# Deferring a fourth norm whose shift is carried as two extra columns, and 512-wide products in all three down projections

## The chip, the cores and the metric

The kernel runs on one core of one Trainium2 chip, in one launch. The metric is device time in microseconds (us), the median of several runs.

## What is computed

Two transformer-like blocks on x of 256 tokens by 1024 features, in fp32. The first block is a state-space mixer, a conv feed-forward (FFN 0), a differential attention and a second conv feed-forward (FFN 1). The second block mixes attention over chosen keys with a gated recurrence, and has a third feed-forward (FFN 2). What matters here is the start of the second block:

```python
mod = jnp.dot(c_act, w_ada[l]) + b_ada[l]
sh1, sc1, ga1, sh2, sc2, ga2 = [m[:, None, :] for m in jnp.split(mod, 6, axis=-1)]
xn = rms_norm_2(h, g_mix[l]) * (1.0 + sc1) + sh1
proj = jnp.dot(xn, w_in[l]) + b_in[l]
q, k, v, qi, ki, wi, xr, yr, gate_a, gate_b = jnp.split(proj, cuts, axis=-1)
```

and each feed-forward's last step, `(silu(gate) * up) @ down_w`, added to the residual stream.

## The kernel before

**Layout.** Activations stand by feature: x is 8 tiles of 128 features by 256 tokens. Every fp32 operand is split into a high and a low part in a reduced fp32 format, and one product of a weight tile (128 x 128) with an activation tile takes three matmuls into one PSUM bank (mm3, L865): low weights by high x, high weights by low x, high by high.

**Weights.** They stream in slabs of 128 x 2048 through a ring of three: SP loads a slab into raw, ScalarE (ACT) writes its high part wh (split_hi, L546, line 553), VectorE (DVE) the low part wl (split_lo, L555, line 567). A high split waits until TensorE (PE) has finished the slab three earlier; SP loads a slab when the low split of the slab three earlier is done. The order of slabs, products and PSUM groups is written out by hand in make_plan (L132) and once more in each engine's program; six PSUM banks are used in turn. Each engine runs its program in order and waits on semaphores.

**Norms.** A norm needs a sum of squares over all features, so over all tiles of x. In the plain form (norm_sum, L1066; norm, L1570 and L2257) PE waits for the sums, turns them into a factor for each token by two transposes (line 1057), and waits until DVE has made xn = x * gain * factor and ACT and DVE have split it. keep_busy matmuls (line 1029) fill part of the wait. In the deferred form (DEFERRED, L354: n1, n2, n3) the next projection runs on the split of x * gain, tile by tile as the residual sums come in (split_tiles, L2295); the sums (norm_squares, L1081, lines 1044 and 1048) and the transposes (norm_factor, L1088) stand among the projection's products, and DVE multiplies the projection's result by the factor.

**Around the change.** FFN 1 ends with the down projection dn1 (stream of kind PAIR3): 8 output tiles in 4 pairs, each pair 3 slabs of 8, 8 and 6 feature tiles, so 22 products for each output tile. residual3 (L2339) adds the results to x on DVE. Behind dn1 stands n4, which has a gain (gs1) and a shift (mod[0:8]) that come from the modulation sums; then the products kk, qi (two slabs, two_slabs takes kk and the first slab of qi together, L873), qi1, vw, qb, yr, xr and eight gate slabs, all from the split of n4's result in xh, xl. The modulation sums are 96 reductions on DVE (ada, L2233, line 2242), two for each step of the table ADA (L339), whose weights POOL loads through a small ring (modulation_weights, L777). In dn2, three of the four pairs already use a form with two matmuls for each product: a 512-wide one of the high weights by high and low activations side by side (line 959), and a 256-wide one of the low weights by the high activations (line 963); DVE adds both halves of the bank.

Of the kernel before, what the change touches and what calls it, by code (L numbers as in the profile page):

```python
# [13 lines left out]
F32 = mybir.dt.float32  # L14
# [324 lines left out]
ADA = {"so": 6, "dn0": 11, "v0": 1, "v1": 1, "v2": 1, "v3": 1, "ao": 2, "dn1": 11, "kk": 1, "qi": 2, "vw": 1, "woa": 2,  # L339
# [14 lines left out]
DEFERRED = {"n1": (1, "ffn_ln0"), "n2": (2, "kv_ln"), "n3": (4, "ffn_ln1")}  # L354
HALVED = ("xbc1", "xbc2", "up2+1")
XN_USES = {0: 0, 5: 1, 6: 2, 7: 3}
# [34 lines left out]
def build_program(nc, io, out):  # L391
    with ExitStack() as ctx:
# [14 lines left out]
        xh = sb("xh", [P, KD, T], F32R)  # L407
        xl = sb("xl", [P, KD, T], F32R)
# [58 lines left out]
        out_done = sem("out_done")  # L467
        (cact_done, ea_done, lam_done, spe_done, pre_done, conv_step, xbc_done, a_done,
# [185 lines left out]
        mh, ml = R(24 * T, 8, T), R(32 * T, 8, T)  # L654
# [13 lines left out]
        mod, gs1, gs2 = S(48), S(8), S(8)  # L668
        negc, posc = S(8), S(8)
# [87 lines left out]
        def _(pool):  # L757
# [78 lines left out]
            pool.wait_ge(xl_done, 8 * 6)  # L836
# [27 lines left out]
        def _(pe):  # L864
# [8 lines left out]
            def two_slabs(slabs, ready):  # L873

                for b, g in slabs:
                    pe.wait_ge(lo_done, b + 1)
                    acquire(pe, g)
                    acquire(pe, g + 1)
                for k in range(KD):
                    ready(k)  # L880
                    for b, g in slabs:
                        for t in range(2):
                            off = k * 256 + t * P
                            mm = mm3(bank(g + t)[:, 0:T],
                                     (wh[:, b % RING, off:off + P], wl[:, b % RING, off:off + P]),
                                     (xh[:, k, :], xl[:, k, :]), k == 0, k == KD - 1, False)
                            if k == KD - 1:
                                mm.then_inc(slab_done if t else half_done, 1)

            def stream(name, X, ready=None, between=None, late=None, deferred=None, factor=True):  # L890
# [6 lines left out]
                def stage(i, j):  # L897
# [37 lines left out]
                    for t in range(tiles):  # L935
# [14 lines left out]
                        if name == "dn2" and i < 3:  # L950
# [514 lines left out]
            for c in range(2):  # L1465
                for k in range(KD):
                    o = k * VW
                    mm = mm3(bank(g)[:, T * c:T * c + VW], (wh[:, b % RING, o:o + VW], wl[:, b % RING, o:o + VW]),
                             (xh[:, k, P * c:P * c + P], xl[:, k, P * c:P * c + P]), k == 0, k == KD - 1, True)
# [13 lines left out]
            for m in range(4):  # L1483
                slab_tile(f"qb{m//2}", m % 2)
# [35 lines left out]
            for s in range(4):  # L1520
                stream(f"yr{s}", (xh, xl))
            for s in range(4):
                stream(f"xr{s}", (xh, xl))
# [5 lines left out]
            for h in range(8):  # L1529
                slab_tile(gate_name(h), 0)  # L1530
# [3 lines left out]
                slab_tile(gate_name(h), 1)  # L1534
# [8 lines left out]
            ffn(2, "n5", 6, 5)  # L1543
# [4 lines left out]
        def _(act):  # L1548
# [11 lines left out]
            def square(r, m, g=None):  # L1560
# [7 lines left out]
                A(sq[:, m % 2, :], x[:, m, :], ACT.Square).then_inc(sq_done, 1)  # L1568

# [20 lines left out]
            def residual(name, r, n, last_of, to=None, first=0, whole=False):  # L1590

                A(warm, eps_t[:, :], ACT.Sqrt)
                for s in range(n + 1 if to else n):
                    if first <= s < (n if to or whole else n - 1):
                        hi(name, s)
                    if to:
                        for m, g in last_of(s - 1):
                            given_back(act, g)
                            A(xh[:, m, :], x[:, m, :], ACT.Copy, scale=vec(DEFERRED[to][1], m)).then_inc(xh_done, 1)
                            square(r, m, g)  # L1600
# [428 lines left out]
            ffn(1, "n3", [], {}, 3, None)  # L2029

            norm("n4", [5], {5: 0})
# [5 lines left out]
            hi("kk", 0)  # L2037
            g = PL.G["kk"]
            wait_tile(act, "kk", 0, 0, 0)
            k0, k1 = bank(g)[low_rows, 0:T], bank(g)[high_rows, 0:T]  # L2040
            biased(kkf[low_rows, 0, :], k0, vec("b_kk", 0)[low_rows, :])
            biased(kkf[high_rows, 0, :], k1, vec("b_kk", 1)[high_rows, :])
            biased(kkf[high_rows, 1, :], k0, vec("b_kk", 0)[low_rows, :])
            biased(kkf[low_rows, 1, :], k1, vec("b_kk", 1)[high_rows, :])
            act.wait_ge(qkv2_done, 4)
            act.sem_inc(free[g % PRING], 1)
            wait_tile(act, "kk", 0, 0, 1)
            biased(kif, bank(g + 1)[:, 0:T], vec("b_ki"))
            act.wait_ge(qkv2_done, 5)
            act.sem_inc(free[(g + 1) % PRING], 1)  # L2050
            for s in range(2):
                hi("qi", s)
                for t in range(2):
                    m, g = 2 * s + t, PL.G["qi"] + 2 * s + t
                    wait_tile(act, "qi", 0, s, t)
                    biased(qif[:, m, :], bank(g)[:, 0:T], vec("b_qi", m))
                    act.wait_ge(qkv2_done, 5 + m + 1)
                    act.sem_inc(free[g % PRING], 1)
# [158 lines left out]
            ffn(2, "n5", [6], {6: 24}, 5, ("wout", 3))  # L2217
# [4 lines left out]
        def _(dve):  # L2222
# [34 lines left out]
            def norm(name, use_gains, k, late=None, early=None):  # L2257
# [7 lines left out]
                for use, gain, shift in use_gains:  # L2265
# [10 lines left out]
                    for m in range(KD):  # L2276
                        V.scalar_tensor_tensor(xn[:, m, :], x[:, m, :], gain(m), bank(g)[:, 0:T],  # L2277
                                               ALU.mult, ALU.mult).then_inc(xn_done, 1)
                        if m and use < 7:
                            low(m - 1)  # L2280
                    if use < 7:
# [7 lines left out]
            def gained_low(use, gain, m, h_, l_):  # L2289

                dve.wait_ge(xh_done, 8 * use + m + 1)
                V.scalar_tensor_tensor(l_[:, m, :], x[:, m, :], vec(gain, m), h_[:, m, :].bitcast(F32),
# [1049 lines left out]
```

## Time and profile before

| | us |
|---|---|
| median of 3 runs | 1148.47 (1147.61 to 1148.58) |
| the profiled execution's own time | 1147.75 |
| its span (first to last instruction) | 1146.0 |
| PE busy in the span | 1127.0 |

The profiled execution takes 1.75 us more than its span and lies 0.72 us under the median of the runs. Line numbers are those of the kernel. A busy PE in these rows is modelled: matmuls are pipelined, and the step from one start to the next is what one costs.

### The profile page before, as it was taken

The page shows a single profiled execution, that of the slowest core. Times are in us where ns is not written, and L with a number is a line of the kernel's source. Part 1 is how long each engine was busy: PE and PEld are TensorE (multiplying, and loading weights), DVE is VectorE, ACT ScalarE, POOL GpSimd, SP SyncE. Part 2 cuts the span into 40 slices and gives each one's busy share as a digit, 9 for nine tenths or more (in the row PEclk, how much of TensorE's full clock was granted, in tenths as well). Part 3 has the DMA queues.
Part 4 walks back from the last instruction along what each step waited for, and adds up shares of the span by engine and source line. Part 5 has one row for each costly group of instructions (what it writes and reads, how often), then busy time and mean ns, then how long its engine had stood idle before and what let it go on. Part 6 is the DMA issues. An engine that isn't in the chain of part 4 may idle for free.

```text
span 1146.0 us, 24061 instructions
## 1 busy us (share of the span) xinstructions
PE 1127.0 (98%) x9194; PEld 1095.8 (96%) x9194; DVE 922.6 (81%) x1608; ACT 699.4 (61%) x1011; POOL 185.1 (16%) x233
## 2 busy tenths in 40 slices
PE   7999999999999999999999999999999999999997
PEld 6999999999999999999999999999988999999987
DVE  5899887788888878877888877679997769888784
ACT  5767885566665457875766653465876347666531
POOL 1000241011112200000111121101324101333310
PEclk9999999999999999999999999999999999999999
DMA  7465456655557864434555578575353655555570
GB/s 268 168 227 186 173 175 246 229 184 183 183 174 275 294 227 151 139 116 144 193 183 183 174 251 302 188 251 180 121 164 118 241 182 173 179 183 183 184 273 37
DMA packets 43713, 220.22 MB, mean 192 GB/s; under 512 B 8063, under 2 KB 12656, under 8 KB 22640
## 3 DMA queue, kind: packets, MB, share of 16 engines
q1 hardware_dynamic: 31552, 185.25, 46.7%
q0 software_dynamic: 9264, 30.94, 7.3%
q10 hardware_dynamic: 2816, 2.90, 0.8%
q8 instruction: 56, 0.92, 0.3%
q14 instruction: 25, 0.20, 0.1%
HBM read 217.97 MB, written 1.11 MB: 191 GB/s over the span
## 4 chain that ended last, share of the span: by engine, by line
PE 90%; DVE 6%; ACT 2%; issue 1%; DMA 0%; DVEq 0%; ACTq 0%
PE ps L870 77%; PE ps L959 3%; DVE wl L567 2%; PE ps L963 1%; ACT wh L553 1%; PE ps_idle L1029 1%; PE ps_idle L1139 1%; PE ps L1500 1%; DVE work L2277 1%; PE ps L1036 0%; DMA x<-in_x 0%; PE ps L1341 0%; PE ps L1477 0%; DVE work L2255 0%; PE ps L1475 0%
## 5 line engine op out<-in xcount | busy, mean ns | idle before, releaser
L870 PE MATMUL ps<-xh,wl 128*128 128x256 f32 x1776 | 509.3, 287 | 1.8 <-DVE xl L2272 1.1
L870 PE MATMUL ps<-xl,wh 128*128 128x256 f32 x1776 | 502.8, 283 | 0.0
L870 PE MATMUL ps<-xh,wh 128*128 128x256 f32 x1776 | 502.6, 283 | 0.0
L567 DVE TENSOR_TENSOR wl<-raw,wh 128x2048 fp32r<-128x2048 f32 (+1 forms) x175 | 394.6, 2256 | 69.6 <-ACT wh L553 68.9
L553 ACT ACTIVATE wh<-raw 128x2048 fp32r<-128x2048 f32 (+1 forms) x178 | 333.2, 1874 | 89.4 <-PE ps L870 69.8
L870 PEld LDWEIGHTS ps<-xh,wl 128*128 128x128 f32 x1776 | 340.7, 192 | 9.2 <-issue 6.7
L870 PEld LDWEIGHTS ps<-xl,wh 128*128 128x128 f32 x1776 | 340.8, 192 | 0.6 <-issue 0.5
L870 PEld LDWEIGHTS ps<-xh,wh 128*128 128x128 f32 x1776 | 340.7, 192 | 0.0
L870 PE MATMUL ps<-actr,wh 128*128 128x256 f32 x1624 | 293.0, 283 | 0.0
L870 PEld LDWEIGHTS ps<-actr,wh 128*128 128x128 f32 x1624 | 253.2, 192 | 0.0
L870 PE MATMUL ps<-actr,wl 128*128 128x256 f32 x812 | 231.3, 285 | 0.5 <-DVE wl L567 0.5
L870 PEld LDWEIGHTS ps<-actr,wl 128*128 128x128 f32 x812 | 155.7, 192 | 1.7 <-issue 1.0
L796 POOL TENSOR_TENSOR actr<-work,actr 128x256 f32 (+1 forms) x66 | 76.8, 1164 | 369.3 <-ACT actr L1855 369.3
L2437 DVE SCALAR_TENSOR_TENSOR work<-work,vecs 128x255 f32<-128x255 f32 (+2 forms) x200 | 85.0, 481 | 1.5 <-POOL work L843 0.9
L1864 ACT ACTIVATE work<-work,vecs 128x256 f32<-128x256 f32 x88 | 52.7, 601 | 38.2 <-DVE work L2702 38.2
L2437 DVE SCALAR_TENSOR_TENSOR work<-ps,vecs,work 128x255 f32<-128x255 f32 (+1 forms) x160 | 67.2, 473 | 10.0 <-ACT work L1864 9.3
L2702 DVE TENSOR_TENSOR work<-ps,work 128x256 f32<-128x256 f32 x88 | 36.9, 421 | 36.5 <-PE ps L870 36.5
L1850 ACT ACTIVATE work<-work 128x256 f32<-128x256 f32 x66 | 27.4, 415 | 54.6 <-DVE work L2437 54.6
L1568 ACT ACTIVATE work<-x 128x256 f32<-128x256 f32 x56 | 22.5, 409 | 56.6 <-DVE x L2369 21.2
L1864 ACT ACTIVATE work<-ps,vecs 128x256 f32<-128x256 f32 x44 | 24.7, 563 | 45.2 <-PE ps L870 45.2
L785 POOL DMA_DIRECT2D work<-in_w_ada x42 | 22.5, 537 | 173.5 <-DVE ada_sum L2242 172.6
L785 POOL DMA_DIRECT2D ada_w<-in_w_ada x54 | 29.1, 539 | 131.0 <-DVE ada_sum L2242 128.9
(279 smaller groups left out, 1231.7 us busy)
## 6 DMA issues: line engine op xcount, KB each, us to landing
raw<-in_up SPq DMA_DIRECT2D x66, 1024.0 KB, 4.9
ada_w<-in_w_ada POOLq DMA_DIRECT2D x54, 256.0 KB, 4.9
raw<-in_xbc SPq DMA_DIRECT2D x12, 1024.0 KB, 5.1
work<-in_w_ada POOLq DMA_DIRECT2D x42, 256.0 KB, 5.2
raw<-in_z SPq DMA_DIRECT2D x8, 1024.0 KB, 5.0
raw<-in_so SPq DMA_DIRECT2D x8, 1024.0 KB, 5.0
raw<-in_dn0a SPq DMA_DIRECT2D x8, 1024.0 KB, 4.9
raw<-in_dn1a SPq DMA_DIRECT2D x8, 1024.0 KB, 5.2
```

The lines of the kernel that those rows point to most:

```text
L553: nc.scalar.activation(wh[:, b % RING, 0:n], raw[:, b % RING, 0:n], ACT.Copy).then_inc(hi_done, 1)
L567: nc.vector.tensor_tensor(wl[:, b % RING, 0:n], raw[:, b % RING, 0:n], wh[:, b % RING, 0:n].bitcast(F32), ALU.subtract).then_inc(lo_done, 1)
L785: pool.dma_start(ada_ring[ada_slot(a)], io["w_ada"][a // 2][:, 512 * (a % 2):512 * (a % 2) + 512])\
L796: nc.gpsimd.tensor_tensor(dst, hbuf[:, j % RING, :], src.bitcast(F32), ALU.subtract)\
L870: mm = nc.tensor.matmul(o, l, r, start=start and n == 0, stop=stop and n == 2)
L959: return nc.tensor.matmul(bank(g), wh[:, r, off:off + P], both, start=k == 0, stop=last)
L963: return nc.tensor.matmul(bank(g)[:, 0:T], wl[:, r, off:off + P], X[0][:, k, :], start=False, stop=False)
L1568: A(sq[:, m % 2, :], x[:, m, :], ACT.Square).then_inc(sq_done, 1)
L1850: A(gsil[:, (j - 1) % RING, :], pre[:, 2 * ((j - 1) % RING), :], ACT.Silu)\
L1864: A(pre[:, 2 * (j % RING) + t, :], src, ACT.Identity, scale=vdyn(f"up_w{f}", 88 + 2 * s + t), bias=vdyn(f"up_b{f}", 2 * s + t))\
L2437: return V.scalar_tensor_tensor(dst[:, d:T], src[:, 0:T - d], w, dst[:, d:T], ALU.mult, ALU.add)
L2702: give_back(V.tensor_tensor(scaled[:, 2 * (j % RING) + t, :], bank(tile_group(up, j, t))[:, 0:T], rstd, ALU.mult), tile_group(up, j, t))
```

## The change

1. n4 is deferred. xh and xl get two more columns for each feature tile (pitch 258 instead of 256 values). kk and the first slab of qi run on the split of x * gs1 with the shift in column 256 (and 257), so that one product gives both the product of the tokens and that of the shift. DVE multiplies the former by the factor into `early` and adds the latter to the bias (early_tile); ACT then makes the same copies as before from there. n4's sums and transposes stand among kk's products.
2. The full n4 result is still made, as mixed (DVE), mixed_high (ACT) and mixed_low (DVE), into ch and cl; qi1, vw, qb, yr, xr and the gates read it there. What lay in that memory (mh, ml, the input of wout) goes to xh, xl.
3. The modulation sums for n4 (first_modulation) go from behind FFN 1 to behind the second weight split of dn1. Four reductions of step qi go to steps qb0 and yr0.
4. dn0 and dn1 take the form of dn2: in three of four pairs two matmuls for each product, and a second add on DVE.

```diff
-ADA = {... "dn1": 11, "kk": 1, "qi": 2, "vw": 1, "woa": 2,
+ADA = {... "dn1": 11, "kk": 1, "vw": 1, "qb0": 1, "yr0": 1, "woa": 2,
-DEFERRED = {"n1": (1, "ffn_ln0"), "n2": (2, "kv_ln"), "n3": (4, "ffn_ln1")}
+DEFERRED = {"n1": (1, "ffn_ln0"), "n2": (2, "kv_ln"), "n3": (4, "ffn_ln1"), "n4": (5, "gs1")}
...
-        xh = sb("xh", [P, KD, T], F32R)
-        xl = sb("xl", [P, KD, T], F32R)
+        xh_wide = sb("xh", [P, KD, T + 2], F32R)
+        xl_wide = sb("xl", [P, KD, T + 2], F32R)
+        xh, xl = xh_wide[:, :, 0:T], xl_wide[:, :, 0:T]
...
-        mh, ml = R(24 * T, 8, T), R(32 * T, 8, T)
+        ch, cl = R(24 * T, 8, T), R(32 * T, 8, T)
+        mh, ml = xh, xl
+        early = W(34 * KB, 4, T)
...
-            pool.wait_ge(xl_done, 8 * 6)
+            pool.wait_ge(xl_done, 8 * 7)
...
+            def shifted_tile(name, t, ready=None, ks=range(KD)):
...
+                    mm = mm3(bank(g)[:, 0:T + 2],
+                             (wh[:, b % RING, off:off + P], wl[:, b % RING, off:off + P]),
+                             (xh_wide[:, k, :], xl_wide[:, k, :]), k == 0, k == KD - 1, False)
...
-                        if name == "dn2" and i < 3:
+                        if kind == PAIR3 and i < 3:
...
-            norm_sum("n4", 4)
-            two_slabs(((PL.S["kk"], PL.G["kk"]), (PL.S["qi"], PL.G["qi"])), x_ready(5))
-            slab_tile("qi1", 0)
-            slab_tile("qi1", 1)
+            pe.wait_ge(shift_low, 1)
+            shifted_tile("kk", 0, x_ready(5))
+            shifted_tile("kk", 1, ks=range(0, 2))
+            norm_squares("n4", 4)
+            shifted_tile("kk", 1, ks=range(2, 6))
+            norm_factor("n4", 4)
+            shifted_tile("kk", 1, ks=range(6, 8))
+            shifted_tile("qi", 0)
+            shifted_tile("qi", 1)
+            slab_tile("qi1", 0, (ch, cl), x_ready(6))
+            slab_tile("qi1", 1, (ch, cl))
```

ACT behind dn1 (split_hi of a slab two ahead is written hi):

```diff
-            norm("n4", [5], {5: 0})
+            hi("kk", 0)
+            norm("n4", [])
+            for m in range(4):
+                mixed_high(m)
+            hi("qi", 0)
+            for m in range(4, KD):
+                mixed_high(m)
...
+            given_back(act, PL.G["kk"])
+            k0, k1 = early[low_rows, 0, :], early[high_rows, 0, :]
...
+            hi("qi", 1)
```

DVE:

```diff
-                                ins = V.tensor_tensor(x[:, m, :], bank(g)[:, 0:T], x[:, m, :], ALU.add)
+                                if p < 3:
+                                    step.add(V.tensor_tensor(x[:, m, :], bank(g)[:, T:2 * T], x[:, m, :], ALU.add))
+                                    step.wait()
+                                ins = V.tensor_tensor(x[:, m, :], bank(g)[:, 0:T], x[:, m, :], ALU.add)
...
-            norm("n4", [(5, lambda m: gs1[:, m:m + 1], lambda m: mod[:, m:m + 1])], 4)
-            lo("kk", 0)
-            for s in range(2):
-                lo("qi", s)
-            lo("vw", 0)
+            ffn(1, ("n3",), 3, to="n4", between=(1, first_modulation))
+            norm_factor("n4", lambda: split_lo(dve, PL.S["qi1"]))
...
+            mixed(0)
+            for m in range(1, KD):
+                mixed(m)
+                mixed_low(m - 1)
+            mixed_low(KD - 1)
...
+            early_tile(0, "kk", 0, [(slice(0, 64), vec("b_kk", 0)), (slice(64, P), vec("b_kk", 1))])
+            early_tile(1, "kk", 1, [(every_row, vec("b_ki"))])
+            split_lo(dve, PL.S["vw"])
+            ada("kk", 0)
+            ada("kk", 0)
+            early_tile(2, "qi", 0, [(every_row, vec("b_qi", 0))])
+            early_tile(3, "qi", 1, [(every_row, vec("b_qi", 1))])
+            split_lo(dve, PL.S["qi1"] + LEAD)
+            split_lo(dve, PL.S["vw"] + LEAD)
+            ada("vw", 0)
+            ada("vw", 0)
```

## Rows read from the trace of the kernel before

**Rows 1.** The page's part 1: busy time, share of the span, instructions of each engine.

```profile
PE 1127.0 (98%) x9194; PEld 1095.8 (96%) x9194; DVE 922.6 (81%) x1608; ACT 699.4 (61%) x1011; POOL 185.1 (16%) x233
```

**Rows 2.** Timeline, PE, end of dn1 to first product behind n4: start, duration (us), instruction.

```profile
725.59 1.02 PE L1029 MATMUL ps_idle<-tri,ident 128*128 128x256 f32 x4
727.15 0.58 PE L1044 MATMUL ps<-tri,work 128*128 128x1 f32 x4 [0.54 <-DVE work L2255]
727.84 0.61 PE L1048 MATMUL ps<-tri,work 128*128 128x1 f32 x4
...
731.36 0.36 PE L870 MATMUL ps<-xh,wl 128*128 128x256 f32 x1 [0.43 <-DVE xl L2272]
731.56 0.28 PE L870 MATMUL ps<-xl,wh 128*128 128x256 f32 x1
```

**Rows 3.** Stretches of time: PE, PEld, DVE, ACT, POOL busy, clock, DMA share, GB/s.

```profile
731.36:757.09 25.73, 25.73 (x218) 25.60 (x218) 16.95 (x31) 15.74 (x20) 4.85 (x9) 1.00 0.62 220
757.00:800.00 43.00, 43.00 (x358) 41.25 (x358) 37.92 (x83) 22.95 (x30) 3.62 (x3) 1.00 0.57 196
405.00:410.00 5.00, 5.00 (x45) 5.00 (x44) 3.00 (x6) 3.61 (x6) 0.00 (x0) 1.00 0.63 215
```

**Rows 4.** Timeline, PE, the deferred norm n2: sums between products.

```profile
408.73 0.50 PE L1044 MATMUL ps<-tri,work 128*128 128x1 f32 x4
...
409.54 0.36 PE L870 MATMUL ps<-xh,wl 128*128 128x256 f32 x1
409.74 0.28 PE L870 MATMUL ps<-xl,wh 128*128 128x256 f32 x1
```

**Rows 5.** Timeline, PE, the deferred norm n1: two transposes between products.

```profile
220.58 0.38 PE L1057 MATMUL ps<-ident,small 128*128 128x128 f32 x2
220.71 0.37 PE L870 MATMUL ps<-xh,wl 128*128 128x256 f32 x1
220.92 0.29 PE L870 MATMUL ps<-xl,wh 128*128 128x256 f32 x1
```

**Rows 6.** Timeline, DVE, end of dn0: tiles 6 and 7 ahead of n2.

```profile
405.94 0.75 DVE L2363 TENSOR_TENSOR x<-ps,x 128x256 f32<-128x256 f32 x2
...
407.64 0.48 DVE L2292 SCALAR_TENSOR_TENSOR xl<-x,vecs,xh 128x256 fp32r<-128x256 f32 x1 [0.22 <-ACT xh L1599]
```

**Rows 7.** Timeline, DVE, the stage behind n4.

```profile
725.68 0.41 DVE L2363 TENSOR_TENSOR x<-ps,x 128x256 f32<-128x256 f32 x1
...
731.13 0.48 DVE L2277 SCALAR_TENSOR_TENSOR work<-x,small,ps 128x256 f32<-128x256 f32 x1
...
735.08 0.47 DVE L2277 SCALAR_TENSOR_TENSOR work<-x,small,ps 128x256 f32<-128x256 f32 x1
...
737.93 2.29 DVE L567 TENSOR_TENSOR wl<-raw,wh 128x2048 fp32r<-128x2048 f32 x1 [0.71 <-ACT wh L553]
...
763.28 0.54 DVE L3013 TENSOR_SCALAR work<-work,small 128x128 f32<-128x128 f32 x2
...
798.85 1.53 DVE L2437 SCALAR_TENSOR_TENSOR work<-work,vecs 128x255 f32<-128x255 f32 x3 [0.46 <-POOL work L843]
```

**Rows 8.** Timeline, ACT, the short weight split of slab vw.

```profile
744.81 1.11 ACT L553 ACTIVATE wh<-raw 128x1088 fp32r<-128x1088 f32 x1 [0.20 <-ACT work L2035]
```

**Rows 9.** The chain that ended last, in dn2: start, duration (us), what.

```profile
1075.16 0.23 PE ps L959
...
1121.74 15.83 PE ps L870 x132
```

**Rows 10.** Timeline, PE, start of dn0: the third slab.

```profile
353.91 0.39 PE L870 MATMUL ps<-actr,wl 128*128 128x256 f32 x1 [0.48 <-DVE wl L567]
```

**Rows 11.** Page, part 5: line, engine, operation, form, count; busy, mean ns; idle before.

```profile
L870 PE MATMUL ps<-xh,wl 128*128 128x256 f32 x1776 | 509.3, 287 | 1.8 <-DVE xl L2272 1.1
```

**Rows 12.** Groups by line and form, DVE: reads off and on a tile's start.

```profile
L2437 DVE SCALAR_TENSOR_TENSOR work<-work,vecs 128x255 f32<-128x255 f32 x96 | 42.4, 479 | 0.9 <-POOL work L843 0.9
...
L2292 DVE SCALAR_TENSOR_TENSOR xl<-x,vecs,xh 128x256 fp32r<-128x256 f32 x24 | 11.1, 479 | 2.0 <-ACT xh L1599 2.0
```

More of the change, by code:

```diff
@@ L334 @@
 PL = make_plan()
-ADA = {"so": 6, "dn0": 11, "v0": 1, "v1": 1, "v2": 1, "v3": 1, "ao": 2, "dn1": 11, "kk": 1, "qi": 2, "vw": 1, "woa": 2,
+ADA = {"so": 6, "dn0": 11, "v0": 1, "v1": 1, "v2": 1, "v3": 1, "ao": 2, "dn1": 11, "kk": 1, "vw": 1, "qb0": 1, "yr0": 1, "woa": 2,
        "dn2": 8}
@@ L871, in mm3 @@
                 return mm
-            def two_slabs(slabs, ready):
-                for b, g in slabs:
+            def shifted_tile(name, t, ready=None, ks=range(KD)):
+                b, g = PL.S[name], PL.G[name] + t
+                if ks[0] == 0:
                     pe.wait_ge(lo_done, b + 1)
                     acquire(pe, g)
[L878 to L888, printed above, removed]
+                for k in ks:
+                    if ready:
+                        ready(k)
+                    off = k * 256 + t * P
+                    mm = mm3(bank(g)[:, 0:T + 2],
+                             (wh[:, b % RING, off:off + P], wl[:, b % RING, off:off + P]),
+                             (xh_wide[:, k, :], xl_wide[:, k, :]), k == 0, k == KD - 1, False)
+                if ks[-1] == KD - 1:
+                    mm.then_inc(slab_done if t else half_done, 1)
             def stream(name, X, ready=None, between=None, late=None, deferred=None, factor=True):
@@ L1597, in residual @@
                         for m, g in last_of(s - 1):
+                            if to == "n4" and m == 0:
+                                shift_columns()
                             given_back(act, g)
[L1599 removed]
+                            A(xh[:, m, :], x[:, m, :], ACT.Copy, scale=gain_of(DEFERRED[to][1], m))\
+                                .then_inc(xh_done, 1)
                             square(r, m, g)
@@ L2344, in residual3 @@
                         lo(name, s)
-                    if between and s == 4:
-                        between()
+                    if between and s == between[0]:
+                        between[1]()
                     if to:
@@ L2978, in modulation @@
                 step.wait()
-            modulation(0, 24)
-            step.add(V.scalar_tensor_tensor(gs1, mod[:, 8:16], 1.0, vec("g_mix", 0, 8), ALU.add, ALU.mult))
-            step.add(V.tensor_scalar(vec("b_ga", 0, 16), vec("b_ga", 0, 16), 0.5, None, ALU.mult))
-            step.add(V.tensor_scalar(vec("b_rg", 0, 16), vec("b_rg", 0, 16), 0.5, None, ALU.mult))
-            step.add(V.tensor_scalar(mod[:, 16:24], mod[:, 16:24], 0.5, None, ALU.mult))
-            step.wait()
-            norm("n4", [(5, lambda m: gs1[:, m:m + 1], lambda m: mod[:, m:m + 1])], 4)
@@ L2988, in _, with first_modulation @@
-            lo("kk", 0)
-            for s in range(2):
-                lo("qi", s)
-            lo("vw", 0)
+            def first_modulation():
+                modulation(0, 24)
+                V.scalar_tensor_tensor(gs1, mod[:, 8:16], 1.0, vec("g_mix", 0, 8), ALU.add, ALU.mult)\
+                    .then_inc(gain_done, 1)
+                step.add(V.tensor_scalar(vec("b_ga", 0, 16), vec("b_ga", 0, 16), 0.5, None, ALU.mult))
+                step.add(V.tensor_scalar(vec("b_rg", 0, 16), vec("b_rg", 0, 16), 0.5, None, ALU.mult))
+                step.add(V.tensor_scalar(mod[:, 16:24], mod[:, 16:24], 0.5, None, ALU.mult))
+                step.wait()
@@ new lines, in _, with mixed, mixed_low @@
+            ffn(1, ("n3",), 3, to="n4", between=(1, first_modulation))
+            norm_factor("n4", lambda: split_lo(dve, PL.S["qi1"]))
+            def mixed(m):
+                V.scalar_tensor_tensor(xn[:, m, :], x[:, m, :], gs1[:, m:m + 1], rstd, ALU.mult, ALU.mult)\
+                    .then_inc(xn_done, 1)
+            def mixed_low(m):
+                dve.wait_ge(xh_done, 8 * 6 + m + 1)
+                V.scalar_tensor_tensor(cl[:, m, :], xn[:, m, :], mod[:, m:m + 1], ch[:, m, :].bitcast(F32),
+                                       ALU.add, ALU.subtract).then_inc(xl_done, 1)
@@ new lines, in _, with early_tile @@
+            mixed(0)
[3 more added lines that the diff above has]
+            mixed_low(KD - 1)
+            def early_tile(n, name, t, biases):
+                g = PL.G[name] + t
+                wait_tile(dve, name, 0, 0, t)
+                for rows, bias in biases:
+                    V.tensor_tensor(early_bias[rows, n:n + 1], bank(g)[rows, T:T + 1], bias[rows, :], ALU.add)
+                give_back(V.tensor_tensor(early[:, n, :], bank(g)[:, 0:T], rstd, ALU.mult), g)
```

101 lines of the change are left out of this document (58 added, 43 removed).

## The prediction

> **What bounds the kernel now.** I read the page's busy times first: PE works 1127.0 of 1146.0 us [rows 1], so only less PE work or a closed PE gap can pay, and another engine counts only where PE waits for it. Then PE's timeline at the end of dn1: the last product is followed at 725.59 by filler matmuls, the sums and the transposes of n4, and the next product starts at 731.36 [rows 2]. That gap of 5.77 us is the largest one in the middle of the kernel. Then the same place at a deferred norm: from 405 to 410, the end of dn0 and n2, PE is busy 5.00 of 5.00 us [rows 3]. Last, the stage behind n4: PE has no gap in 731.36 to 757.09 while DVE works 16.95 of 25.73 us; in 757 to 800 DVE works 37.92 of 43.00 us, so there it has little room [rows 3]. The clock is 1.00 of full (2.4 GHz) throughout these stretches [rows 3].
>
> **The down projections.** A product by two matmuls: 3 pairs x 2 tiles x 22 = 132 products from 1075.16 to 1121.74, 46.58 / 132 = 0.3529 us; by three: 132 matmuls, so 44 products, in 15.83 us, 0.3598 us each [rows 9]. The gain is 0.0069 us a product, 132 x 0.0069 = 0.91 us in dn1. In dn0 PE waits 0.48 us at 353.91 for the low split of the third slab [rows 10]; that split comes from up0's last tile and ACT's work, not from PE's first two slabs, so what PE gains in their 32 products (0.22) it waits longer there: 0.91 - 0.22 = 0.69. Together **1.60**. By the Trainium skill's "TensorE: Matmul & The Clock Gate", section "Wait — 56ns, not 53.3ns?", a warm matmul costs its columns plus some 2.5 ns; an estimate from that is one such 2.5 ns saved a product, 0.66 us over 264 products, where the rows give 1.82 before the wait. I keep to the rows, which are this very form.
>
> The second add, six on each dn, costs DVE one add of 0.41 [rows 7], some 0.9 us a pair with its step wait. It delays the low split two slabs ahead, which has a slab of slack: nothing, and if that cover is gone, up to 0.9 a pair. The six small operations of the modulation sums come behind dn1's second split and delay the third by about 1 us, in the same cover; the work that they stood in front of, n4's chain, is lighter by as much. The deferred splits of n4 (8 on ACT, 8 on DVE) lie in dn1 as n2's do in dn0.
>
> **n4 on PE.** E is PE's end of dn1 (725.59 before). Behind E the first tile of kk runs at once if the split of tiles 6 and 7 is there: at n2 the low split of tile 7 ends 407.64 + 0.48 - 405.94 = 2.2 us after the first add [rows 6], and that add comes 0.1 after E [rows 7]. PE wants tile 7 at E + 7 x 0.36 = 2.5: no wait, as at n2. The gap goes: +5.77. The first product behind a pause costs 0.20 instead of 0.12 [rows 2]: +0.08. What stays among the products: sums 408.73 to 409.54, 0.81, and 0.08 on the product behind them [rows 4]; transposes 0.13, and 0.09 on the product behind [rows 5]. 96 matmuls have two more columns: 96 x 2 / 2400 = 0.08. So 5.77 + 0.08 - 0.89 - 0.22 - 0.08 = **4.66**.
>
> **The new wait.** qi1 now waits for the full n4 result in ch, cl, tile by tile. PE reaches it after 96 products' matmuls (96 x 0.1197 = 11.5, plus 1.2 for the norm): E + 12.7, and wants tile 7 at 15.2. DVE: sums on PE end near E + 4.5, root and reciprocal by 5.1, then the low split of qi1, 2.2 [rows 7], the copy of the factor, and the first mixed tile at about 7.8. A tile took 3.95 / 5 = 0.79 (731.13 to 735.08 are five) [rows 7]; ACT's hop included, the first low part starts near 8.85, the eighth ends near 8.85 + 5.5 + 0.5 = 14.9. Between tiles 3 and 4 ACT splits vw, 1.11 [rows 8], of which DVE's lead takes most: the eighth ends at 14.9 to 15.5. I take a wait of **0.2** (0 to 0.4); below nothing it can't go, PE would just run on. Behind qi1, vw's low split follows eight mixed tiles and two early tiles, near E + 17.7, PE wants it at 18.6; that of qb0 comes near 22.4, wanted at 24.3. These are thin covers: each us that DVE is late beyond 0.9 is a us of PE.
>
> **Queues.** DVE gets the factor's copy, four early products and five bias adds, under 10 x 0.42 = 4.2 us, against 8.8 us of idle time in this stage [rows 3]. POOL's wait for the eight low parts moves from the early to the late n4, so its two gate loads and the eight reduction loads behind them come some 4 us later after E; the reductions were moved back too, and their users stand on DVE with idle time in front. SP loads the slab behind qi1 7 us earlier, that behind vw about 4 earlier, while PE comes 4.5 earlier. Scores start at 763.28, 6.2 us behind PE's first qb tile [rows 7, 3]; I get 5.6 after, and two reductions more (1.2) in the first yr step: DVE is 0.6 later against PE in 757 to 800, and 798.85 has 0.46 of slack that absorbs most of it [rows 7], the next recurrent tile as much. Cost nothing, bound 0 to 1.
>
> **Sum.** 1.60 + 4.66 - 0.2 = 6.1 off the profiled execution's 1147.75 (span 1146.0): 1141.7. It lies 0.72 under the median shown, so the median goes from 1148.47 to **1142.4**, 0.53% faster. Bounds of these terms: 4.7 (0.4 and 1 lost) to 6.7 off (no wait, 0.2 less lost in dn0, 0.2 of reading error), and 0.9 for the spread of a few runs: 1140.8 to 1143.8.
>
> **The rivals.**
> 1. The wait moves to qi1 or vw. The chain of two splits, the mixed tiles and early tiles has no slack at qi1 and 0.9 at vw; one split late (2.2) and the reading errors make some 3 us of PE wait: 1145.4. For it: eight tiles on two engines with a split between. Against: DVE's 8.8 us of idle time in the stage [rows 3].
> 2. The down projections give nothing, because the second adds push the splits late: 1142.4 + 1.6 = 1144.0. For it: 0.9 us a pair more on DVE. Against: dn2 runs in the same form without a PE gap and with costlier adds [rows 9].
> 3. Slower, by the pitch of xh and xl. 258 values put every odd feature tile 8 bytes off a 16-byte start, and PE reads these tiles as moving data all over the kernel: 3 x 1776 = 5328 matmuls [rows 11], less 912 that now read ch, plus 192 of wout, 4608, half of them odd: 2304. If such a read costs more than 6.1 / 2304 = 2.7 ns, the change is a loss. No row shows PE reading off such a start. The nearest rows are DVE's: reads one or more values off a tile's start take 479 ns for 255 values, on the start 479 for 256 [rows 12]. So I take nothing; the far bound is the 13 ns by which a matmul (0.1199 us) exceeds its 256 columns at 2.4 GHz (0.1067), paid once more: 30 us, a time of 1172. The Trainium skill speaks for this rival: "SBUF — State Buffer", section "Door 1: The DMA port swizzle", says that SBUF has 16-byte lines and that an access crossing to a new one pays a penalty; a slice off the start touches 65 lines instead of 64. Rows 12 show no such price on DVE, and no run here shows PE's.
> 4. Nothing beyond noise: the gap is closed and reappears further on, in the top-k stretch where DVE works 37.92 of 43.00 us [rows 3], so that PE waits in the gate stage for what it won: 1147.
>
> **How the numbers follow.** Forecast 0.68; rival 1 0.15; rival 2 0.07; rival 3 0.05; rival 4 0.05. A measurement of this kernel can tell 0.2% (2.3 us) from no change, so faster means under 1146.2: forecast, rivals 2 and nearly all of 1, 0.89; same is rival 4 and the rest of 1, 0.06; slower 0.05. The forecast's own range is 1140.8 to 1143.8; with rival 2 and half of rival 1 it reaches 1145.4, and leaves out under 2 in 10.
>
> **What would show it.** Right: PE's timeline without a gap at the end of dn1, kk's first product directly behind dn1's last; dn0 and dn1 with steps of 0.353 us and the wait at dn0's third slab grown to 0.7; at most 0.4 us of wait in front of qi1; 258-wide matmuls with a step under 0.122 us. Wrong: waits of PE on mixed_low, on the low splits of vw or qb0, longer waits on the attention transposes of the gate stage, or a mean step above 0.120 us in the up projections, which would be the pitch.

## The result, and the profile after

The changed kernel takes 1135.54 us (median of 3 runs, 1135.54 to 1136.73) where the kernel before took 1148.47: 12.9 us less, a ratio of 0.9897 with the interval 0.9883 to 0.9911 (the quotient of the two medians, 0.9887, lies in it). Forecast were 1142.4, 6.1 us less. Faster was right, but the time lies below the whole range.

Page, part 1, of the changed kernel (answers to [rows 1]):

```profile
PE 1112.8 (98%) x8916; PEld 1071.0 (94%) x8916; DVE 932.7 (82%) x1639; ACT 702.6 (62%) x1020; POOL 183.9 (16%) x233
```

PE's busy time fell by 14.2 us and the span from 1146.0 to 1133.8 by 12.2, so the time in which PE is not busy grew by 2.0. The rows below show both: PE faster where nothing was changed, and new waits behind n4.

**The seam at n4 is closed, at the times forecast.** Timeline of PE from the end of dn1 (answers to [rows 2, 4, 5]):

```profile
717.39 0.40 PE L880 MATMUL ps<-actr,wh 128*128 128x256 f32 x2
717.63 0.28 PE L880 MATMUL ps<-xh,wl 128*128 128x258 f32 x1
...
721.25 0.50 PE L1053 MATMUL ps<-tri,work 128*128 128x1 f32 x4
721.61 0.58 PE L1057 MATMUL ps<-tri,work 128*128 128x1 f32 x4
722.06 0.37 PE L880 MATMUL ps<-xh,wl 128*128 128x258 f32 x1
...
723.61 0.38 PE L1066 MATMUL ps<-ident,small 128*128 128x128 f32 x2
723.74 0.36 PE L880 MATMUL ps<-xh,wl 128*128 128x258 f32 x1
...
730.34 0.28 PE L880 MATMUL ps<-actr,wl 128*128 128x256 f32 x1
```

E, PE's end of dn1, is 717.63 here. kk's first product (258 wide) starts there, directly behind dn1's last: the 5.77 us are gone. The sums take 722.06 - 721.25 = 0.81 and the transposes 0.13, as forecast from [rows 4, 5]. qi1's first product (its operand is now in actr) starts at 730.34 = E + 12.71, forecast E + 12.7, without a wait. The 258-wide matmuls step at 0.121 us (91 distances), forecast under 0.122.

DVE in the same stage (answers to [rows 6, 7]):

```profile
719.48 0.49 DVE L2322 SCALAR_TENSOR_TENSOR xl<-x,small,xh 128x256 fp32r<-128x256 f32 x1 [0.22 <-ACT xh L1622]
...
732.22 0.48 DVE L3040 SCALAR_TENSOR_TENSOR actr<-work,small,actr 128x256 fp32r<-128x256 f32 x1 [0.18 <-ACT actr L2057]
...
733.69 1.28 DVE L569 TENSOR_TENSOR wl<-raw,wh 128x1088 fp32r<-128x1088 f32 x1
...
737.89 2.29 DVE L569 TENSOR_TENSOR wl<-raw,wh 128x2048 fp32r<-128x2048 f32 x1 [0.89 <-ACT wh L555]
...
751.86 0.69 DVE L2272 CUSTOM_DVE_ANT_0 ada_w<-ada_w,cact 128x512 f32<-128x512 f32 x1 [3.65 <-DMA ada_w<-in_w_ada]
...
753.09 0.69 DVE L2272 CUSTOM_DVE_ANT_0 ada_w<-ada_w,cact 128x512 f32<-128x512 f32 x1 [0.54 <-DMA ada_w<-in_w_ada]
...
753.71 0.55 DVE L3092 TENSOR_SCALAR work<-work,small 128x128 f32<-128x128 f32 x2
```

The last low split of n4 ends at 719.97 = E + 2.3 (forecast 2.2), the eighth mixed low part at 732.70 = E + 15.1 (14.9 to 15.5), vw's split at E + 17.3 (17.7), qb0's at E + 22.6 (22.4). All thin covers held. Then come two waits that the forecast did not have: DVE stands 3.65 and 0.54 us in front of the two reductions that the change put at qb0, until their loads land. The scores behind them start at 753.71, 12.3 us behind PE's first qb tile (741.41); before it was 6.2, forecast 5.6.

What the loads wait for stands in the chain of waits of the same kernel. The first reduction of step vw ends at 744.62. POOL issues the two loads at 744.93 and 745.54; the second lands at 753.07, 7.5 us after its issue, and the first lets DVE go on at 751.86, 6.9 us after its own (by the page, the median landing of these loads is 5.2):

```profile
744.93 0.54 POOL ada_w L795
...
745.54 7.53 DMA ada_w<-in_w_ada
```

In the kernel before, DVE stood in front of reductions of this stage for their loads too, there with a weight split between them and the scores:

```profile
759.70 0.69 DVE L2242 CUSTOM_DVE_ANT_0 ada_w<-ada_w,cact 128x512 f32<-128x512 f32 x1 [1.93 <-DMA ada_w<-in_w_ada]
```

And PE's waits in 700 to 840 us (engine, line, what it waited for: total, times, longest):

```profile
PE ps L880 <- ACTq L2111: 1.0, 1, 1.0
PE ps L1516 <- DVE work L3139: 0.7, 1, 0.7
PE ps L1516 <- DVE work L2480: 0.5, 1, 0.5
PE ps L1350 <- DVE work L3189: 0.4, 1, 0.4
```

2.6 us in all, none of them in the kernel before: there PE's waits from 700 to 845 are 0.5 and 0.4 us at n4 itself [rows 2]. The first is a PSUM bank that ACT gives back late, because its relu waits 5.5 us for DVE's scores. At dn0's third slab PE waits 0.76 us (0.48 before [rows 10], forecast 0.7):

```profile
349.98 0.50 PE L968 MATMUL ps<-actr,wh 128*128 128x512 f32 x1 [0.76 <-DVE wl L569]
```

**PE is faster in up projections that the change does not touch.** The chain that ended last, of before (up0, up2) and then of after (up0, up2, and the last narrow products of dn2, which answer to [rows 9]):

```profile
220.96 120.98 PE ps L870 x1008
...
953.94 121.22 PE ps L870 x1008
```

```profile
218.16 119.84 PE ps L880 x1008
...
943.26 120.11 PE ps L880 x1008
...
1109.70 15.67 PE ps L880 x132
```

120.98 / 1008 = 0.1200 us a matmul before, 119.84 / 1008 = 0.1189 after, the same instructions with the same shapes. In before, the distance of two starts in these stretches is 120.0 ns throughout (standard deviation under 0.7 ns from 240 to 330 us); in after it changes from 113 to 125 ns, with a mean of 118.9. Over some 8000 such matmuls 1 ns is 8 us. If the edit of xh and xl did this, it works in the direction opposite to rival 3; the first two experiments ask.

### The profile page after: what moved, and what is told of

Read it like the earlier page. It is cut to its first block, busy times and chain, and to the rows that moved or that the text cites. A ratio compares the mean times of both kernels' runs of the same rounds, so it can differ in the third digit from the quotient of the medians.

```text
span 1133.8 us, 23542 instructions
## 1 busy us (share of the span) xinstructions
PE 1112.8 (98%) x8916; PEld 1071.0 (94%) x8916; DVE 932.7 (82%) x1639; ACT 702.6 (62%) x1020; POOL 183.9 (16%) x233
## 4 chain that ended last, share of the span: by engine, by line
PE 81%; DVE 12%; ACT 4%; issue 2%; DMA 2%; POOL 0%; DVEq 0%; ACTq 0%
PE ps L880 62%; PE ps L968 7%; DVE wl L569 4%; PE ps L972 4%; ACT wh L555 2%; DMA ada_w<-in_w_ada 1%; PE ps_idle L1148 1%; DVE work L3109 1%; DVE work L2480 1%; DMA work<-running_sums 1%; PE ps_idle L1038 1%; DVE m8s L3107 0%; DVE work L2307 0%; PE ps L1516 0%; PE ps L1045 0%
## 5 line engine op out<-in xcount | busy, mean ns | idle before, releaser
L880 PE MATMUL ps<-xh,wl 128*128 128x256 f32 (+1 forms) x1536 | 435.4, 283 | 1.5 <-DVE xl L2322 0.7
L880 PE MATMUL ps<-xh,wh 128*128 128x256 f32 (+1 forms) x1536 | 433.3, 282 | 0.0
L880 PE MATMUL ps<-xl,wh 128*128 128x256 f32 (+1 forms) x1536 | 431.6, 281 | 0.0
L880 PEld LDWEIGHTS ps<-xh,wl 128*128 128x128 f32 x1536 | 289.2, 188 | 4.1 <-issue 2.5
L880 PEld LDWEIGHTS ps<-xl,wh 128*128 128x128 f32 x1536 | 290.2, 189 | 0.5 <-issue 0.5
L880 PEld LDWEIGHTS ps<-xh,wh 128*128 128x128 f32 x1536 | 290.3, 189 | 0.0
L880 PEld LDWEIGHTS ps<-actr,wh 128*128 128x128 f32 x1576 | 242.0, 188 | 0.2
L880 PE MATMUL ps<-actr,wl 128*128 128x256 f32 x788 | 225.3, 286 | 1.0 <-ACTq L2111 1.0
L880 PEld LDWEIGHTS ps<-actr,wl 128*128 128x128 f32 x788 | 148.4, 188 | 6.5 <-issue 6.1
L968 PE MATMUL ps<-actr,wh 128*128 128x512 f32 x396 | 138.3, 394 | 0.8 <-DVE wl L569 0.8
L972 PE MATMUL ps<-actr,wl 128*128 128x256 f32 x396 | 108.9, 282 | 0.0
L968 PEld LDWEIGHTS ps<-actr,wh 128*128 128x128 f32 x396 | 73.3, 188 | 16.7 <-DVE wl L569 1.1
L972 PEld LDWEIGHTS ps<-actr,wl 128*128 128x128 f32 x396 | 74.4, 188 | 1.5
```

The costliest lines, as they stand in the source:

```text
L880: mm = nc.tensor.matmul(o, l, r, start=start and n == 0, stop=stop and n == 2)
L968: return nc.tensor.matmul(bank(g), wh[:, r, off:off + P], both, start=k == 0, stop=last)
L972: return nc.tensor.matmul(bank(g)[:, 0:T], wl[:, r, off:off + P], X[0][:, k, :], start=False, stop=False)
```

## The experiments

Fourteen kernels, in the order of the questions. Ratios are against runs of the kernel before on the same chip, whose medians there were 1147.5 to 1147.8 us. A value is 4 bytes. By the sizes in the kernel before, wh, wl, x, xh, xl and actr follow each other in sizes that are multiples of 8192 bytes, so that the weights and every operand tile lie at the same place modulo 512 bytes.

**1. The pitch alone (e1_pitch), and a shift without a pitch (e2_shift).** Before, with

```diff
+        xh_wide = sb("xh", [P, KD, T + 2], F32R)     # e1: also xl; xh, xl = their first T columns
```
```diff
+        pad = sb("pad", [P, 32])                     # e2: 128 unused bytes between xl and actr
```

> The kernel before with nothing but the layout of the change: xh and xl get the pitch of 258 values, and by it all tensors allocated behind them (actr, work and so on) move by 64 and 128 bytes; the two columns stay unused. Theory A (layout): the changed kernel's up0 runs 1008 matmuls in 119.84 us where the kernel before took 120.98, with the same instructions, so the matmuls gain 1.1 ns each from where their operands lie; some 7800 products' matmuls in all, so 1140 to 1142, and up0 near 119.85. Theory B (the gain of 12.9 us is the deferral and the wide products, more than I summed): 1148 to 1149, up0 near 121.0. Rival 3 of the prediction (the pitch costs): slower than 1150.

> The kernel before with 128 unused bytes behind xl: xh and xl keep the pitch of 256, actr and all that lies behind it move by 128 bytes as in the changed kernel. If the place of actr alone makes its matmuls faster: the products read from actr (2436 matmuls with a step of 119.9 ns before) fall to 118.7 ns and those read from xh stay at 119.9; 1145 to 1146. If the pitch is what counts: nothing changes, 1148 to 1149. If it is something else that the whole program shares (chip, clock): all products as before and 1148 to 1149 too, told apart by e1.

Measured: e1 1139.48 us, ratio 0.9926 (0.991 to 0.9943), so 8.1 us less with no change of the work. e2 1144.71, 0.9979 (0.9969 to 0.9989), 2.9 less. The chain of e1 (up2; end of dn2), then of e2:

```profile
947.60 120.09 PE ps L871 x1008
...
1114.03 15.67 PE ps L871 x132
```

```profile
950.84 121.22 PE ps L871 x1008
...
1118.39 15.67 PE ps L871 x132
```

e1 has both rows of after. In e2 xh and xl stayed, and actr moved with all that lies behind it: up2, which reads xh and xl, is what it was before (121.22), and dn2, which reads actr, is what it is in after (15.67 instead of 15.83). So a pitch is not needed; it is enough here that an operand starts 128 bytes further, and the gain goes to the matmuls that read it.

**2. The wide form and the deferral at the new places (e3_narrow, e5_ada).** e3 is the changed kernel with dn0 and dn1 narrow again; e5 is the changed kernel with the reductions one step later each:

```diff
-                        if kind == PAIR3 and i < 3:
+                        if name == "dn2" and i < 3:          # e3, and no second add in dn0, dn1
```
```diff
-ADA = {... "vw": 1, "qb0": 1, "yr0": 1, ...
+ADA = {... "vw": 1, "qb1": 1, "yr1": 1, ...
```

> The changed kernel with dn0 and dn1 back to three 256-wide matmuls a product; the wide form stays in dn2. By the prediction's sum: 1.6 us slower than the changed kernel, 1137.1. By the steps in the changed kernel's own trace (wide pair 231 + 119.5, narrow 3 x 118.7 ns, 264 products): 5.6 ns each, 1.5 us, less 0.2 at dn0's third slab: 1136.8. If the wide form does nothing there (rival 2): 1135.5.

> The changed kernel with the two reductions of step qb0 moved to step qb1 and the two of yr0 to yr1, so that they come a weight split later and DVE does not stand 4.2 us in front of the scores for their loads. If the 2.6 us of new PE waits behind n4 (a bank at qb, the recurrent gates, the attention transposes) come from that: 1133 to 1134.5. If they come from DVE's work as such or from ACT: 1135 to 1136. If the loads are then late in the top-k stretch, where DVE has least room: slower, 1136 to 1138.

Measured: e3 1137.62, ratio 0.9913 (0.9896 to 0.9929); against the change's 0.9897 the wide form is worth 0.0016, 1.8 us, which is about the reach of either interval, and against e1 the deferral alone only 1.9. e5 1133.22, ratio 0.9873 (0.9857 to 0.989): 2.3 us under the changed kernel. In e5's timeline of DVE the last reduction at vw is followed by no other, and the scores start:

```profile
745.58 0.69 DVE L2272 CUSTOM_DVE_ANT_0 ada_w<-ada_w,cact 128x512 f32<-128x512 f32 x1
...
749.15 0.54 DVE L3092 TENSOR_SCALAR work<-work,small 128x128 f32<-128x128 f32 x2
```

Scores start 6.75 us behind the first qb tile (742.40) instead of 12.3, and the view of waits has no wait of PE in 700 to 840 us. So the place of the moved reductions causes the new waits. Of the 5.5 us by which the scores come earlier, 4.2 are the two waits for loads and most of the rest is the reductions' own work.

**3. The change without the new places (b4_old_places, b5_old_places_ada).** The changed kernel with xh and xl as before, the 258-wide operand in free memory of the work buffer; b5 with e5's edit on top:

```diff
+        with nc.sbuf_tensor("ahead", [P, 29 * 256], F32), \
+                nc.sbuf_tensor("kx", [P, 2, KD, T + 2], F32R) as kx:
+            xh_wide, xl_wide = kx[:, 0, :, :], kx[:, 1, :, :]
         work = sb("work", [P, FN])
```

> The changed kernel with xh and xl back at a pitch of 256 values and every operand of the products at the very place that it has in the kernel before; the operand with the two more columns (kk and two tiles of qi alone) lies in a part of the work buffer that is free there, and the early products elsewhere in it. Wide down projections, deferral and the reductions at qb0 and yr0 stay. Theory (three parts that add: places -8.1, wide form -1.8, deferral -1.9 with the reductions where the change puts them): products at 120.0 ns again, and 1147.5 - 3.7 = 1143.8 us (1143.0 to 1144.8). Rival A (the gain of e1_pitch and that of the rest overlap, so that without new places little is left): 1145.5 to 1147.5. Rival B (the wide form or the deferral gains more at the old places): below 1142.5.

> b4_old_places with the reductions of e5_ada (qb1 and yr1 in place of qb0 and yr0). Theory (the sum of the prediction, 6.1 us, was right for what it summed, but for the waits that the reductions bring): 1147.5 - 6.1 = 1141.4 us (1140.6 to 1142.3), and no wait of PE between 745 and 805. Rival A (the reductions moved on gain only at the new places): as b4_old_places, 1143.8. Rival B (a part of the deferral's gain came from the places): 1142.6 to 1143.8.

Measured: b4 1144.04, ratio 0.9962 (0.9949 to 0.9976); b5 1141.50, ratio 0.9947 (0.9933 to 0.996). Both as the theory had them. b5 has no wait of PE in 700 to 840; b4 has

```profile
PE ps L882 <- ACTq L2114: 1.4, 1, 1.4
PE ps L1493 <- ACT work L2099: 0.4, 1, 0.4
```

and in both up0 and up2 step at 0.120 again. So the parts add, within intervals that reach 1.5 to 2 us to either side: places 8.1, wide form and deferral 6.2 if the reductions stand well, less 2.5 for where the change puts them: 11.8 us, against 11.8 by the ratio of the changed kernel (0.0103 x 1147.6).

**4. Which places? (k4_shift32, k1_shift64, k2_shift512, k3_weights).** The kernel before with unused bytes, or with small tensors that it has anyway, ahead of xh, of actr, or of wl and xl:

```diff
+        pad_x = sb("pad_x", [P, 8])      # k4: ahead of xh; k1: 64 bytes there and 192 ahead of actr
```

> The kernel before with 32 unused bytes a partition ahead of xh, so that xh, xl and actr all start 32 bytes later, modulo 8192, than wh and wl do; the pitch of xh and xl stays 256 values, no product is changed. Theory (any offset between the places where weights and moving operand lie ends the lock of the steps at 120.0 ns): the matmuls that read xh, xl and actr step at 118.7 to 119.0 ns, and the time is near that of the run in which only the pitch was changed, 1139.5 us (1138 to 1142). Rival A (a shift must be 128 bytes or more, as it was for actr): steps stay at 120.0 and the time at 1147.6 +- 0.7. Rival B (what counts is that neighbouring feature tiles lie at different places, so a pitch is needed): actr at 118.7 or 120.0, xh at 120.0, the time 1144.7 at best.

> The kernel before with 64 unused bytes ahead of xh and 192 ahead of actr: xh and xl lie 64 bytes behind wh and wl modulo 8192, actr 256 bytes. Theory (any offset): both families at 118.7 to 119.0 ns, 1139.5 us (1138 to 1142). Rival A (the offset must differ between xh and xl too, since high and low parts are read in turn): xh stays at 120.0, actr at 118.7, 1144.7 us. Rival B (only 128 does it for actr): everything at 120.0, 1147.6.

> The kernel before with two tensors of 512 bytes that it has anyway allocated ahead of xh and ahead of actr: xh and xl lie 512 bytes behind wh and wl modulo 8192, actr 1024. Theory in its simplest form (any offset): 118.7 to 119.0 ns for both, 1139.5 us (1138 to 1142). Rival A (what counts is the offset modulo a smaller power of two, 512 or less): both at 120.0, 1147.6. Between them (modulo 1024): xh at 118.9, actr at 120.0, some 1142.

> The kernel before with 128 unused bytes ahead of wl and 128 ahead of xl: against wh, wl and xh lie 128 bytes on, xl and actr 256; so xh lies as wl does but not as wh, and no moving operand lies as wh does. Theory (what counts is the moving operand against the weights that are loaded beside it): products of xh and xl at about 119 ns, those with wl by xh perhaps at 120, actr at 118.7; 1138 to 1143 us. Rival A (what counts is the moving operand's own start, or that of high against low moving operand, not the weights): xl now differs from xh, so xh and xl near 118.9 and actr near 118.7, 1139.5. Rival B (a pitch is needed for xh): xh at 120.0, 1144.7.

Measured, with the offset from the weights and the mean distance of two starts:

| Kernel | xh, xl | Step, ns | actr | Step, ns | us | Ratio (interval) |
|---|---|---|---|---|---|---|
| before | 0 | 119.9 | 0 | 119.8 | 1147.5 | |
| k2_shift512 | 512 | 119.9 | 1024 | 119.8 | 1147.52 | 1.0003 (0.9994 to 1.0013) |
| e2_shift | 0 | 119.9 | 128 | 118.8 | 1144.71 | 0.9979 (0.9969 to 0.9989) |
| k1_shift64 | 64 | 117.5 | 256 | 119.8 | 1138.66 | 0.9927 (0.991 to 0.9944) |
| k4_shift32 | 32 | 117.0 | 32 | 116.8 | 1127.81 | 0.982 (0.9803 to 0.9836) |
| k3_weights | 128 and 256 | 117.5 | 256 | 119.0 | 1135.84 | 0.9893 (0.9875 to 0.9911) |

The theory (any offset, 118.7 to 119.0) fell both ways: 512 and 256 bytes do nothing, and 32 bytes do far more than the pitch did, 19.7 us with eight values of padding. k3, where low weights lie 128 bytes off the high ones, gives xh a gain that neither offset alone foretold; with the two weights apart no simple rule came out.

**5. The step by itself (m1_offsets, m2_offsets).** PE alone, 120 matmuls a section, each section with its own line:

```diff
+                for a in steps(8, 0, 0): mm = nc.tensor.matmul(*a[:3], start=a[3], stop=a[4])   # operand, wh, wl start
```

> Nothing of the reference is computed: the tensors lie as in the kernel before, weights and actr are filled with a constant, and PE alone runs sections of 120 matmuls each, three a k as in the products (low weights by high operand, high weights by low operand, high by high), five tiles a section, with no DMA and no other engine at work; each section has its own line, and moves the start of the operand in actr, or of the weights, by so many values. Theory (the step of a matmul depends on where its operand lies against its weights, by itself, without any traffic beside it): the section without an offset steps at 120.0 ns, 8 values (32 bytes) at 116.7, 16 at 117.5, 32 at 118.8, 64 and 128 at 119.8 to 120.0; weights and operand moved together (8, 8, 8) at 120.0. Rival A (it depends on the absolute place of the operand, not on that of the weights): moved weights alone change nothing, operand and weights moved together give 116.7. Rival B (it is contention with transfers and the other engines' accesses, which the layout only steers): every section steps alike, whatever the offset.

The chain of m1 (start, duration, line, matmuls). Operand offsets in values: L476 0, L478 8, L480 16, L481 20, L483 32, L485 48, L488 64, L492 112; L495 the weights by 8; L499 operand and weights by 8; L506 a pitch of 258:

```profile
39.63 14.40 PE ps L476 x120
...
68.28 14.00 PE ps L478 x120
...
96.47 14.13 PE ps L480 x120
110.61 14.40 PE ps L481 x120
...
139.41 14.24 PE ps L483 x120
...
167.88 14.13 PE ps L485 x120
...
210.28 14.39 PE ps L488 x120
...
267.18 13.60 PE ps L492 x120
...
309.55 14.20 PE ps L495 x120
...
366.53 14.39 PE ps L499 x120
...
466.68 14.19 PE ps L506 x120
```

14.40 / 120 = 120.0 ns, 14.00 is 116.7, 13.60 is 113.3. No transfer of data and no other engine is at work, so it is not contention (rival B falls). Moving the weights by 8 values shortens the step too (L495, 14.20, as the operand at 56 values, 8 short of 64, line 486), and moving both together restores it (L499): what counts is the place of the operand against that of its weights (rival A falls). 64 values are as slow as 0, and so are 128 and 192 (14.38 and 14.40, lines 493 and 494): the slow place comes back every 256 bytes. It is not the only one: 20 values (L481) and 24 (line 482) take 14.40 as well, so that 80 and 96 bytes gain nothing.

> As the run m1_offsets (nothing of the reference is computed; PE alone, sections of 120 matmuls), with other starts of the operand: 112 values three times with other sections between, its neighbours, starts that are the same modulo 64 values, and operand tiles at a pitch of 258 values with low parts 64 bytes further, as in the changed kernel. Theory (the step follows from the offset alone, so it comes back each time): 112 values step at 113.3 ns all three times and 8 values at 116.7, as in m1_offsets; at a pitch of 258 values, 118 to 119 whatever the start, since eight tiles go through offsets that differ by 56 bytes. Rival (the pattern is a lock that a section falls into by its history): 112 values give 113.3 in one section and 117 to 118 in another, and equal sections differ by over 1 ns.

The chain of m2: L476 and L480 112 values, L479 8, L483 110, L490 48, L493 6, L495 2:

```profile
38.46 13.62 PE ps L476 x120
...
80.08 14.00 PE ps L479 x120
94.08 13.62 PE ps L480 x120
...
136.09 14.40 PE ps L483 x120
...
234.66 13.60 PE ps L490 x120
...
275.86 14.41 PE ps L493 x120
...
304.58 14.40 PE ps L495 x120
```

112 and 8 values come back to 0.2 ns. But 48, 112, 176, 240 and 368 values are the same place modulo 256 bytes: here all of them give 113.3 to 113.5, while m1 has 113.3 at 112 and 117.75 at 48 (14.13 / 120), in one run. So one place can have two steps, and the place alone does not settle it; that it is what ran before, as the rival has it, is not shown. A pitch of 258 stays at 118.4 to 120.3 in all of its 18 sections, where 118 to 119 was expected. That its eight tiles go through fast and slow places alike would explain it, but is not shown.

**6. The best place in the kernel, and all together (k5_shift448, b3_all).** k5 is the kernel before with 448 bytes (112 values) ahead of xh; b3 is b5 with these 448 bytes and narrow products in all three down projections:

```diff
+        ada_sum = sb("ada_sum", [P, 96])        # moved here from behind work
+        pad_x = sb("pad_x", [P, 16])
         xh = sb("xh", [P, KD, T], F32R)
```

> The kernel before with 448 bytes ahead of xh (a tensor of 384 bytes that it has anyway, and 64 unused ones), so that xh, xl and actr all start 112 values behind wh and wl; the pitch stays 256. Theory (the section of 112 values of m1_offsets holds in the kernel too): products at 113.3 ns instead of 120.0 over some 8000 matmuls, 53 us at most, of which the stages in which DVE sets the pace keep some: 1095 to 1115 us. Rival A (113.3 needs a chip without traffic): steps like those of 48 values, 117.75, and 1130 +- 4 us. Rival B (beyond some point another engine becomes the bound): steps of 113.3 in the up and down projections, but new waits of PE on DVE, and 1115 to 1128 us.

> b5_old_places_ada with xh, xl and actr 448 bytes further, as in k5_shift448, and narrow products in all three down projections, dn2 too (at these places three narrow steps are 340 to 353 ns a product, the wide form 353). Theory (places and deferral add): k5_shift448 was 1119.9, less 4.5 for the deferral and 0 to 2 for the narrow products in dn2: 1113 to 1116 us. Rival A (with PE faster by 5 per cent DVE is the bound behind n4, and the deferral's gain turns into waits there): 1117 to 1120. Rival B (the narrow products fall into slower steps in the down projections): 1116 to 1119 with steps of 117.8 in dn0, dn1 or dn2.

Measured: k5 1119.86, ratio 0.977 (0.9735 to 0.9805), slower than the 1095 to 1115 of the theory. The chain of k5, up1 with dn1 and up2:

```profile
535.16 170.03 PE ps L871 x1500
...
934.79 114.53 PE ps L871 x1008
```

170.03 / 1500 = 113.3 ns, but up0, dn0 and the stage from 750 to 780 us step at 117.8, constant to 0.7 ns: two levels, each held for a whole stretch, at the same offset. The mean steps are 115.3 on xh and xl and 116.3 on actr; over some 7600 matmuls this is 17 us more than at 113.3, so most of what is missing from the 53. PE's waits on DVE grew by little (2.2 us on the attention transposes, 0.8 before).

b3 1113.34, ratio 0.9701 (0.9684 to 0.9717): 34.4 us less than before and 22 less than the change, in the range of the theory. Its chain, up0 and up2 with part of dn2, and its only wait of PE in 700 to 840:

```profile
216.57 114.28 PE ps L883 x1008
...
922.18 181.17 PE ps L883 x1536
```

```profile
PE ps L1353 <- DVE work L3196: 1.2, 1, 1.2
```

up0 is at 113.4 here, and up2 to dn2 at 117.9: the levels fell otherwise than in k5.

## Why the prediction was right and wrong

- **Down projections, 1.60: right, as far as can be told.** 1.8 was measured (after against e3), with intervals that overlap. The steps say the same: a product by two matmuls takes 0.351 us in after and 0.352 in b5 (mean of 358), where 0.353 was taken from dn2, and the third slab's wait grew to 0.76 as forecast. The second adds made no new wait of PE in dn0 or dn1, so rival 2 falls.
- **n4 on PE, 4.66, and the new wait, 0.2: right.** With the reductions moved and the old places (b5) the whole change is worth 6.2 us; 6.1 was the sum. qi1 came at E + 12.7 and had no wait at all; rival 1, a wait at qi1 or vw, falls.
- **"Their users stand on DVE with idle time in front ... Cost nothing, bound 0 to 1": wrong by 2.5 us.** The step moved four reductions and looked only at DVE's idle time in front of them. The ring has two slots in this stretch, so a load is issued when the reduction two places ahead has freed its slot: vw's reductions end at 744.62 and 745.24, and DVE reaches qb0's a split later, at 748.2, while the loads take 6.9 and 7.5 us to land. The idle time in front of DVE's reductions before was in part itself such a wait (the 1.93 us at 759.70). It is rival 4's kind of loss (the gain comes back as PE waits further on), but not in its size: 2.6 us, at a bank of qb, the recurrent gates and the attention transposes. The last of these was among the prediction's own signs of being wrong.
- **"So I take nothing" for the pitch of xh and xl: wrong by 8.1 us, the largest error, and the reason that the time lies outside the range.** Rival 3 saw that the edit moves the operands of thousands of matmuls, and bounded it only from above, by 13 ns a matmul. "Below nothing" was left out without a reason, though a step of 120.0 ns, 13.3 above the columns' time, leaves room below as well; all four rivals are slower than the forecast, and none stood for a time under the range. The nearest rows, DVE's [rows 12], say nothing of a matmul. The mechanism was wrong too: what the runs show at work is the place of every operand against its weights, not a price on odd tiles. So the count missed actr, which the edit moves by 128 bytes and from which 2.9 of the 8.1 us come (e2). The price was not 2.7 ns more but 1.1 less.
- The Trainium skill's "SBUF — State Buffer" ("Door 1: The DMA port swizzle") was weighed there with an access that pays for each new 16-byte line. The sections of m2 do not settle it. Starts of 2 and 6 values, off a line's start, take 14.40 and 14.41, as the start without an offset, so against that they cost nothing. But 110 and 114 values, off a line's start, take 14.40 and 14.41 beside 13.62 at 112; and 108 and 116, which are on one, take 14.31 and 14.29. Whether lines have a part beside the place against the weights is not shown.
- The Trainium skill's "TensorE: Matmul & The Clock Gate" ("Wait — 56ns, not 53.3ns?") would put 256 columns at 109.2 ns, an estimate from its figure; no section of m1 or m2 came below 113.3.

Together: 6.1 forecast, plus 8.1 that was priced at nothing, less 2.5 for waits that were priced at nothing too, makes 11.7; the ratio says 11.8.

## What to carry to other kernels

Where an edit moves a buffer that matmuls read, price the move with both signs, and look at the step of the matmuls: one that is well above its columns' time is worth a trial of a few offsets, 32 bytes first, before any work on the schedule (k4: 19.7 us, more than the whole change; 256 and 512 bytes gave nothing). Where loads go through a ring, a reader that is moved forward is costed from the reader that frees its slot, plus the landing time at that place (6.9 and 7.5 us here, 5.2 in the median), not from the idle time in front of it. And a part that is to be measured by itself is measured at the old places of everything else.

## What the runs showed of the hardware

- The step of a matmul of 256 columns with its weight load depends on where its operand lies against its weights in memory: 120.0 ns at the same place modulo 256 bytes, 116.7 at 32 bytes, 117.8 at 64, 118.7 at 128, 113.3 to 113.5 at 448, and 120.0 again at 80 and 96, at a granted clock of 0.997 in m1 and 0.999 in m2 (2.4 GHz), with no other engine at work. Why is not shown by any run.
- At 448 bytes (and at 192, the same modulo 256) there are two levels, 113.3 and 117.8 ns, and a long unbroken stretch keeps one of them (k5, b3; 48 and 112 values in m1). What decides between them stays open, as does the rule where high and low weights lie apart (k3).
- At 448 bytes the wide form loses its gain: in k5's dn2 a product by two matmuls steps at 0.3531 us, three narrow ones at 113.3 to 117.8 take 0.340 to 0.353.
